# A decoder step's expert stage: dense batches ranked first, one-hot gate groups inside sequences five to eight, last query steps behind the last sequence

## The reference, cut to what matters

```
def block(tb):                                   # 128 tokens
    q = (tb @ wq).reshape(PEER_BLOCK, PEER_HEADS, 2, PEER_QHALF)
    sc = jnp.einsum('thpd,hpnd->thpn', q, keys).astype(jnp.float32)
    s1, i1 = lax.top_k(sc[:, :, 0], PEER_TOPK)
    s2, i2 = lax.top_k(sc[:, :, 1], PEER_TOPK)
    cand = (s1[..., :, None] + s2[..., None, :]).reshape(...)
    cidx = (i1[..., :, None] * PEER_KEYS + i2[..., None, :]).reshape(...)
    top_s, top_p = lax.top_k(cand, PEER_TOPK)
    eidx = jnp.take_along_axis(cidx, top_p, axis=-1)
    g = jax.nn.softmax(top_s, axis=-1)
    act = jax.nn.gelu(jnp.einsum('td,thkd->thk', tb, u_tab[eidx]))
    w = (g * act.astype(jnp.float32)).astype(tb.dtype)
    return jnp.einsum('thk,thkd->td', w, v_tab[eidx])
```

## Time and profile before

| | |
|---|---|
| median of three runs | 3616.84 us (3608.49 to 3617.91) |
| the profiled execution, span | 3614.2 us (its own device time is not given apart from the span) |
| PE busy | 3393.9 us (94%) |
| DVE busy | 2625.2 us (73%) |
| POOL busy | 2070.1 us (57%) |
| ACT busy | 841.3 us (23%) |
| first block of the expert stage | about 672 to 1494 us |
| second block | 1494.67 us to the end |

### The profile page before, as it was taken

One profiled execution on the slowest core, in us unless ns is written; L12 is line 12 of the kernel. 1 busy time (PEld: TensorE's weight loads), 2 busy tenths in 40 slices (PEclk: granted clock), 3 DMA queues, 4 the chain that ended last, 5 costly groups with the idle time before them and its releaser, 6 DMA issues.

```text
span 3614.2 us, 41476 instructions
## 1 busy us (share of the span) xinstructions
PE 3393.9 (94%) x12615; PEld 1771.0 (49%) x12615; DVE 2625.2 (73%) x5427; ACT 841.3 (23%) x1785; POOL 2070.1 (57%) x1636
## 2 busy tenths in 40 slices
PE   8999799899899987999999999999999999999888
PEld 5676564444444444644444444444444444444343
DVE  3344573278777875578887888887888788888884
ACT  2332560244334335311111111111111111111021
POOL 0000100058888888567777777776777677777540
PEclk9999899999999986999999999999999999999999
DMA  4100613478888885999999999999999999999961
GB/s 147 35 23 15 266 75 105 150 196 215 210 217 217 216 208 126 308 366 407 406 406 396 404 404 399 403 393 406 399 400 400 398 389 407 405 404 395 355 215 42
DMA packets 410615, 1023.34 MB, mean 283 GB/s; under 512 B 93965, under 2 KB 130030, under 8 KB 406834
## 3 DMA queue, kind: packets, MB, share of 16 engines
q0 software_dynamic: 221184, 604.27, 46.0%
q1 hardware_dynamic: 175138, 394.69, 31.5%
q10 hardware_dynamic: 14096, 22.02, 1.7%
HBM read 972.05 MB, written 48.77 MB: 282 GB/s over the span
## 4 chain that ended last, share of the span: by engine, by line
DMA 22%; POOL 17%; issue 8%; DVE 7%; PE 4%; ACT 0%; DVEq 0%; SPq 0%; ACTq 0%
DMA u<-in_peer_u,idx_all 21%; POOL v L2134 9%; POOL u L2126 8%; DVE u L2144 2%; DVE facc L2172 2%; PE e_b L2288 1%; PE e_b L2059 1%; DVE wq L2172 1%; PE e_b L2027 1%; DMA w_room<-x_scratch 1%; DVE k_room L2074 1%; PE e_b L2276 0%; DVE ln_st L964 0%; DVE w_room L2358 0%; DVE act L2144 0%
## 5 line engine op out<-in xcount | busy, mean ns | idle before, releaser
L2126 POOL DMA_INDIRECT u<-in_peer_u,idx_all x576 | 727.0, 1262 | 390.8 <-DVE act L2144 260.1
L2059 PE MATMUL e_b<-w_room,e_room 128*128 128x512 f32 x2048 | 910.2, 598 | 24.8 <-DVE k_room L2074 16.3
L2144 DVE CUSTOM_DVE_ANT_0 u<-u,xb 128x1024 f32<-128x1024 f32 x576 | 705.3, 1225 | 299.4 <-DMA u<-in_peer_u,idx_all 291.4
L2027 PE MATMUL e_b<-wq 128*128 128x512 f32 x2048 | 900.4, 592 | 0.0
L2134 POOL DMA_INDIRECT v<-in_peer_v,idx_all x576 | 696.1, 1208 | 216.1 <-issue 174.5
L1756 POOL DMA_INDIRECT gate_scratch<-e_room,slot_of x384 | 611.6, 1593 | 201.8 <-issue 117.5
L2059 PEld LDWEIGHTS e_b<-w_room,e_room 128*128 128x128 f32 x2048 | 391.2, 192 | 524.7 <-issue 491.8
L2027 PEld LDWEIGHTS e_b<-wq 128*128 128x128 f32 x2048 | 379.5, 190 | 429.2 <-issue 429.2
L2172 DVE SCALAR_TENSOR_TENSOR facc<-v,w,facc 128x1024 f32<-128x1024 f32 x317 | 406.6, 1283 | 1.4
L2172 DVE SCALAR_TENSOR_TENSOR wq<-v,w,wq 128x1024 f32<-128x1024 f32 x254 | 325.7, 1282 | 0.5
L2020 ACT ACTIVATE wq<-e_b 128x512 f32<-128x512 f32 x256 | 139.0, 594 | 712.0 <-PE e_b L2013 712.0
(11 more groups left out here) (380 smaller groups left out, 3609.5 us busy)
## 6 DMA issues: line engine op xcount, KB each, us to landing
wq<-in_peer_u SPq DMA_DIRECT2D x128, 512.0 KB, 9.7
w_room<-in_peer_v SPq DMA_DIRECT2D x128, 512.0 KB, 10.3
w_room<-in_cache_k SPq DMA_DIRECT2D x192, 256.0 KB
w_room<-in_cache_v SPq DMA_DIRECT2D x160, 256.0 KB
gate_scratch<-zeros SPq DMA_DIRECT2D x24, 1024.0 KB, 26.6
u<-in_cache_v SPq DMA_DIRECT2D x96, 256.0 KB
wq<-gate_scratch SPq DMA_DIRECT2D x96, 256.0 KB, 16.6
u<-in_cache_k SPq DMA_DIRECT2D x64, 256.0 KB
```

The source lines that it names most:

```text
L2027: last = pe.matmul(AQ[c % 2][:, 0:DT], UT[c % 2][:, k, :], x1Td[:, k, :], start=(k == 0), stop=(k == KC - 1))
L2059: last = pe.matmul(OQ[i % 2][b][:], WT[n % 2][:, c, m * P:m * P + P], Vd[(4 * n + c) % NVD][:, b * 512:b * 512 + 512], start=(c == 0), sto ...
L2126: pool.indirect_dma_start(u[x % NU], None, a["peer_u"], bass.IndirectOffsetOnAxis(ap=idx_all[:, t, h, j:j + 1], axis=0)).then_inc(s_u[x % ...
L2144: dve.tensor_tensor_reduce(u[x % NU], u[x % NU], xb[t % 2][:], 1.0, 0.0, ALU.mult, ALU.add, act16[k % 2][:, j:j + 1]).then_inc(s["ufree"], 1)
```

## The change

The batches are ordered dense first: batches 0 to 7 are the dense group's heads, 8 to 15 the gathering group's, so each batch uses another head's weights and the ring is refilled after every batch. Splitting and quads move from the tail into the sequences with index 4 to 7 (the fifth to the eighth): the split to slot 140, one quad in each of eight slots (20, 22, 23, 25, 26, 28, 29, 31) of each of them, with one PSUM bank and one staging buffer in place of two. In these sequences the q matmuls are thinned to 21, and what is left of them stands in the tail, from `MIXED` to `S_TURN` + 1. The planner gets a room for VectorE of its own in seven slots of the tail. The turned indices take the place of the dense batches' indices in SBUF, no longer of the scores of attention.

```diff
-        jT = S[:, 0:4 * P].rearrange("p (n t) -> p n t", n=4)
-        sqb = S[:, 4 * P:6 * P].rearrange("p (t e) -> p t e", t=2)
+        jT = i_room[0].rearrange("p (n t) -> p n t", n=4)
+        sqb = i_room[1][:, 0:2 * P].rearrange("p (t e) -> p t e", t=2)
...
-        gst = [v_flat[:, n * PK * GB:(n + 1) * PK * GB] for n in (1, 0)]
+        gst = v_flat[:, PK * GB:2 * PK * GB]
...
-        HOT = [B[3], B[7]]
+        HOT = B[3]
...
         def q_pe(pe, e, y):
             m, k = y // KC, y % KC
-            h, group = e // 2, e % 2
+            group = e // PH
             if y == 0:
-                pe.wait_ge(s_wq[h % NR], 16 * (h // NR + 1))
+                pe.wait_ge(s_wq[e % NR], 16 * (e // NR + 1))
...
-            last = pe.matmul(B[m][:], ring[h % NR][:, k, m * P:m * P + P], x1T[group][:, k, :],
+            last = pe.matmul(B[m][:], ring[e % NR][:, k, m * P:m * P + P], x1T[group][:, k, :],
...
-        SPLIT, NQUAD = MIXED, P // 4
-        QUAD_AT, q = {}, 0
-        while q < NQUAD:
-            x = max(QUAD_AT, default=MIXED + 1) + 1
-            n = min(3 if x <= MIXED + 8 else 2, NQUAD - q)
-            QUAD_AT[x] = range(q, q + n)
-            q += n
-        MADE_AT = {x: [q + 2 for q in qs if q + 2 < NQUAD] for x, qs in QUAD_AT.items()}
-        MADE_AT[MIXED + 1] = [0, 1]
+        SPLIT, NQUAD = 4 * SEQ_SLOTS + 12, P // 4
+        QUAD_SLOTS = (20, 22, 23, 25, 26, 28, 29, 31)
+        QUAD_AT, MADE_AT = {}, {SPLIT + 1: [0, 1]}
+        for q in range(NQUAD):
+            x = (SPLIT // SEQ_SLOTS + q // len(QUAD_SLOTS)) * SEQ_SLOTS + QUAD_SLOTS[q % len(QUAD_SLOTS)]
+            QUAD_AT[x] = [q]
+            if q + 2 < NQUAD:
+                MADE_AT[x + 1] = [q + 2]
...
+        Q_LAST = {MIXED: 4, MIXED + 1: 4, O_NORM: 8, O_TURN: 3, O_MIX - 1: 2, O_MIX + 1: 8}
+
+        def q_steps(x):
+
+            c = x % SEQ_SLOTS
+            if x >= MIXED:
+                return Q_LAST.get(x, 0 if x < S_TURN + 1 else 2)
+            if x < 5 or 16 <= c < 20:
+                return 3
+            if x == 6 or c % 8 == 7 or c in (3, 11, 27):
+                return 0
+            if x >= 4 * SEQ_SLOTS:
+                return int(c % 2 == 0 and c < 12 or c in (21, 24, 30))
+            return 1
...
+        DVE_ROOM = {MIXED + 1: 1.5, O_NORM: 0.0, O_TURN: 1.5, O_TURN + 1: 4.0, O_MIX - 1: 4.0, O_MIX: 4.0, O_MIX + 1: 0.0}
...
-                while used + 1.3 * len(MADE_AT.get(slot, ())) >= 2.5 or (slot < MIXED and slot % SEQ_SLOTS in (16, 17)):
+                while (used + 1.3 * len(MADE_AT.get(slot, ())) >= DVE_ROOM.get(slot, 2.5)
+                       or (slot < MIXED and slot % SEQ_SLOTS in (16, 17))):
...
         def scatter_pool(pool, h):
 
-            pool.wait_ge(s["tk"], 2 * h + 1)
+            pool.wait_ge(s["tk"], h + 1)
...
         def split_pe(pe):
-            pe.wait_ge(s["tk"], 2 * (PH - 1) + 1)
-            pe.wait_ge(s["O"], DB)
+            pe.wait_ge(s["tk"], PH)
...
-            wait(pe, s["ge"], q - 1)
-            if q == 1:
-                pe.wait_ge(s["Oe"], DB)
+            wait(pe, s["ge"], q)
...
-                if e % 2 and m:
-                    refill(act, e // 2)
+                if m:
+                    refill(act, e)
```

More of the change, by code:

```diff
@@ L1154, in peer @@
         gd = carve([P, NDT, PH, TOPK])
-        i12d = [carve([P, NDT, PH, TOPK]) for n in range(2)]
+        i_room = [carve([P, NDT * PH * TOPK]) for n in range(2)]
+        i12d = [x.rearrange("p (m h k) -> p m h k", m=NDT, h=PH) for x in i_room]
         i12 = carve([P, 2, UN, TOPK])
@@ L1232, in peer @@
         s_gs = [sem(f"s_gs{n}") for n in range(NSC)]
-        s_gst = [sem(f"s_gst{n}") for n in range(2)]
+        s_gst = sem("s_gst")
         s_xn = [sem(f"s_xn{n}") for n in range(UN)]
@@ L1343, in score_pe @@
                         last = pe.matmul(B[2][:, at:at + PK], qTt[e % 2][:, m, i * P:i * P + P],
-                                         keysT[:, 2 * (e // 2) + m, :], start=True, stop=True)
+                                         keysT[:, 2 * (e % PH) + m, :], start=True, stop=True)
                     else:
@@ L1423, in rank_index_dve @@
                 rule, ids, val = ALU.is_equal, iota[0:R, 0:TOPK], tif[0:R, :, 1, :]
-            dst = i12d[n][:, :, e // 2, :] if e < NBAT and e % 2 == 0 else work(e).i12[0:R, n]
+            dst = i12d[n][:, :, e, :] if e < PH else work(e).i12[0:R, n]
             ch.sync()
@@ L1670, in peer @@
         Q_AT, Q_DONE = {}, {}
+        Q_LAST = {MIXED: 4, MIXED + 1: 4, O_NORM: 8, O_TURN: 3, O_MIX - 1: 2, O_MIX + 1: 8}
[10 more added lines that the diff above has]
+            return 1
         x, step = Q_FIRST, 0
         while step < NBAT * 2 * KC:
-            c = x % SEQ_SLOTS
-            n = 3 if x < 5 or 16 <= c < 20 else 0 if c % 8 == 7 or c in (3, 11, 27) or x == 6 else 1
-            for _ in range(min(n, NBAT * 2 * KC - step)):
+            for _ in range(min(q_steps(x), NBAT * 2 * KC - step)):
                 e, y = step // (2 * KC), step % (2 * KC)
@@ L1806, in quad_pe @@
                 pe.wait_ge(s["jT"], 2)
-            wait(pe, s["ge"], q - 1)
-            if q == 1:
-                pe.wait_ge(s["Oe"], DB)
+            wait(pe, s["ge"], q)
             for t in range(4):
-                last = pe.matmul(HOT[q % 2][:].rearrange("p (e t) -> p t e", t=4)[:, t, :], oh[q % NOH][0][:, t, :],
+                last = pe.matmul(HOT[:].rearrange("p (e t) -> p t e", t=4)[:, t, :], oh[q % NOH][0][:, t, :],
                                  oh[q % NOH][1][:, t, :], start=True, stop=True)
@@ L1817, in quad_act @@
             if n == 0:
-                act.wait_ge(s["qe"], 2 * NBAT)
-                wait(act, s_gst[b % 2], 16 * (b // 2))
+                wait(act, s_gst, 16 * b)
             act.wait_ge(s["gq"], q + 1)
-            dst = gst[b % 2].rearrange("p (e t) -> p e t", t=GB)[:, :, 4 * n:4 * n + 4]
-            act.activation(dst, HOT[q % 2][:].rearrange("p (e t) -> p e t", t=4), ACT.Copy).then_inc(s["ge"], 1)
+            dst = gst.rearrange("p (e t) -> p e t", t=GB)[:, :, 4 * n:4 * n + 4]
+            act.activation(dst, HOT[:].rearrange("p (e t) -> p e t", t=4), ACT.Copy).then_inc(s["ge"], 1)
             if n == GB // 4 - 1:
                 act.wait_ge(s["ge"], q + 1)
-                act.dma_start(rows(hot_d, b * PK, PK), gst[b % 2]).then_inc(s_gst[b % 2], 16)
+                act.dma_start(rows(hot_d, b * PK, PK), gst).then_inc(s_gst, 16)
         def fold_pe(pe):
@@ L1937, in first_act @@
                 act.wait_ge(s["qs"], x - S_Q + 1)
-                refill(act, PH + x - S_Q)
+                refill(act, NBAT + x - S_Q)
             if x in (S_Q + UN, S_Q + 2 * UN):
@@ L1950, in first_act @@
             if x == SPLIT + 1:
-                for q in MADE_AT[x]:
+                for q in (0, 1):
                     quad_hot_act(act, q)
@@ L1995, in load_g @@
             if n == 0:
-                for b in range(2):
-                    sp.wait_ge(s_gst[b], 16 * P // GB // 2)
+                sp.wait_ge(s_gst, 16 * P // GB)
             src = hot_d.rearrange("(b p) (c t) -> p b c t", p=PK, t=GB)[:, :, 4 * n:4 * n + 4, :]
```

7 lines of the change are left out of this document (3 added, 4 removed).

## The result

The changed kernel is slower. Four runs of it gave 3633.29 to 3649.27 us, median 3644.72; four of the kernel before a median of 3617.38. The ratio is 1.0067, with a 95% interval of 1.0050 to 1.0085: 27 us at the medians. The forecast was 3616 with a range to 3630, and "slower by over 0.3%" had a chance of 0.10.

The account below looks back on a forecast made before the run. GpSimd's unbroken chain of 384 scatters was taken to set the second block's start; everything else was hidden before its end, and the start came 0.5 us sooner: 3616.84 - 0.5 gives 3616.3, said as 3616, range 3604 to 3630.

Parts of the forecast that it names:

- I take nothing: Attention sequences: eight more 1 MB weight loads are hidden and cost 0 us; DMA share rises from 0.88 to about 0.92.
- The upper bound of 16 us: Added weight loads: at most 4 us in each of four sequences, if the pages waited for all of it.
- A sequence as now, 81 us; bounds 75 and 85: Sequences with index 4 to 7: quads in and q matmuls out leave each at 81 us, between 75 and 85.
- The last sequence, 81 us at full clock: Last attention sequence: quads and q matmuls bring full clock, so it takes 81 us and ends about 1358 us, not 1371.9.
- T: Time at which attention's last values come: forecast about 1358 us, bounds 1350 and 1380, against 1371.9 before.
- The tail: After attention's last values: VectorE ends 107 to 121 us after T, at 1465 to 1479 us, before the scatters end.
- the 55 us of ranking: End of the tail: VectorE ranks from batch 14's fourth top to batch 15's end, 25.2 + 30.1 us.
- Rival B: Tail: VectorE's ranking of batches 14 and 15 becomes the end if T is over 1372 to 1386; up to 3640 us; chance 0.09.
- The scatters as a floor: End of first block: GpSimd's 384 scatters run without a break to 1486.7 us, so the second block begins at 1494.2 us.

Follow-up runs that it names:

- e1: The kernel before with only the dense-first batch order and a ring load after every batch; quads and q matmuls as before: 3641.3 us, ratio 1.0068.
- e5: e1 without the ring loads after even batches, so one load a sequence as in the kernel before: 3619.2 us, ratio 1.0005.
- e7: The kernel before in its own order, with each head's weights loaded twice, once for each of its two batches: 3634.0 us, ratio 1.0048.
- e3: The changed kernel with all ring loads kept, those after batches 0 to 12 held back to slot 20 or 21 of a sequence: 3627.0 us, ratio 1.0029.
- e6: e1 with all its ring loads kept, those of batches 0 to 12 held back to early in the values half: 3623.6 us, ratio 1.0022.
- e8: The kernel before with 336 of 384 scatters, each head's last two choices left out: 3615.2 us, ratio 0.9996.
- e9: The kernel before with SyncE's last nine issues moved to the head of the second block's SyncE stream: 3613.3 us, ratio 0.9989.
- e4: The changed kernel with the split and the 32 quads back in the tail: 3724.6 us, ratio 1.0294.

## Why the prediction was wrong, by its own steps

**"I take nothing" for the eight loads: the step that failed.** They cost 22 us (e1 - e5) or 16 us (e7 against its own before), and moving them took 18 us off the changed kernel (e3). The working had three parts. That a load lands long before it is needed was right, and beside the point: who waits is not the user of the weights but TensorE, for pages that the load displaces. That the DMA share goes from 0.88 to 0.92 was right to the digit (e6), and it was an average: the share was 0.94 where the load was put and 0.20 after the softmax. The upper bound of 16 us took all eight loads to lie in the first four sequences, as the first eight batches do. But every batch refills the ring, the gathering ones too, so only four of them lie there. The loads in sequences 4 to 6 of the kernel before, of e1 and of the changed kernel:

```profile
wq<-in_peer_wq ACTq DMA_DIRECT2D x3, 1024.0 KB, 9.6
```
```profile
wq<-in_peer_wq ACTq DMA_DIRECT2D x7, 1024.0 KB, 7.9
```
```profile
wq<-in_peer_wq ACTq DMA_DIRECT2D x4, 1024.0 KB, 5.4
```

The rate behind the bound, 4 us a load, would have covered e1: eight loads, 22 us. It was counted for four of them, and then set to nothing.

**"A sequence as now, 81 us; bounds 75 and 85": failed, 89.4.** Of the 25.0 us that sequences 4 to 6 grew, 5.4 go when the loads are moved (e3, 262.7); the changed kernel has only one load more there. The quads and the thinned q table are most of the rest: e3 against e6, which differ in these and the tail's plan, gives 262.7 - 243.9 = 18.8 us in sequences 4 to 6 and 7.0 in sequence 7. TensorE's work is indeed no more (e3 226.7 us busy, e6 226.1). But the prediction looked for the wait in the wrong place: no quad waits for VectorE. TensorE's waits in the changed kernel's sequences 4 to 6:

```profile
PE e_b L1535 <- ACT w_room L1545: 16.3, 21, 3.5
PE e_b L1626 <- ACT w_room L1613: 7.7, 15, 1.5
```

and in the same sequences of the kernel before:

```profile
PE e_b L1535 <- ACT w_room L1545: 5.5, 10, 1.9
...
PE e_b L1626 <- ACT w_room L1613: 3.7, 6, 1.5
```

Attention is a give and take between TensorE and ScalarE: each turned page is copied out before TensorE can go on. The q matmuls were what TensorE did meanwhile. Thinned in the keys half, they leave TensorE waiting for the copies (16.3 for 5.5 us). In the values half there was no room for a quad. Windows of a values half and a keys half before:

```profile
1165.90:1196.30 30.40, 29.48 (x169) 14.48 (x171) 22.21 (x113) 8.44 (x17) 25.52 (x17) 1.00 0.85 207
1196.30:1246.80 50.50, 44.87 (x266) 23.87 (x259) 41.24 (x137) 26.09 (x55) 42.27 (x28) 1.00 0.93 233
```

and after:

```profile
1190.20:1233.00 42.80, 37.80 (x235) 22.95 (x233) 28.12 (x132) 23.84 (x55) 35.78 (x24) 0.92 0.79 194
1233.00:1279.40 46.40, 38.86 (x220) 19.95 (x221) 15.88 (x22) 24.71 (x52) 39.08 (x25) 0.93 0.96 265
```

TensorE was busy for 29.48 of 30.40 us in the values half, so what is added there lengthens it. It grew by 12.4 us: TensorE is busy 8.3 us longer, with eight quads of 1.13 us in, fewer q matmuls and a granted clock of 0.92, and idle 4.1 us longer beside a ScalarE that works three times as much (23.84 for 8.44 us). The keys half, 6 us of TensorE lighter (38.86 for 44.87), gives back 4. The prediction had netted the two halves against each other as if work could flow between them.

**The last sequence, 81 us at full clock: failed.** It took 103 us (1318.26 to 1421.60), with a granted clock of 0.77 in its second half. More work at a better clock took longer than less work at the low one. T came 64 us later than forecast, 1421.6 for 1358, and over 40 past the upper bound.

**The tail: the total right, its parts not.** From T, VectorE was to end after 107 to 121 us; it ended after 111.3 (1532.87). LayerNorm was over at T + 39.8 (forecast 49), the samples' queries were done at T + 89.5. But the 55 us of ranking behind it did not run through. Timeline of ScalarE and VectorE:

```profile
1492.12 0.60 ACT L1357 ACTIVATE e_room<-e_b 128x512 f32<-128x512 f32 x1 [24.26 <-PE e_b L1326]
...
1502.18 0.26 ACT L1437 ACTIVATE e_room<-e_room 128x64 f32<-128x64 f32 x1
...
1502.47 0.22 DVE L1456 TENSOR_REDUCE zx<-e_room 128x4 f32<-128x64 f32 x1 [15.36 <-ACT e_room L1437]
```

VectorE stood 15.4 us for ScalarE's exponentials of batch 14's gates (L1437). ScalarE goes through its slots in order, and ahead of that instruction it had waited 24.3 us for TensorE's sample queries. A LayerNorm that was over 9 us sooner and a wait of 15 us that the forecast did not have offset each other for the most part: that the total came out is in part luck. The tail shrank by 11 us in the changed kernel, and by 20 in e3 against e6, and that is paid for before it starts.

**Rival B named the new end, not what moved T.** It had VectorE's ranking as the last link, from T over 1372 to 1386, at one us for each us, and T went 35 to 50 us past that point. What it gave as the reason, quads that wait for VectorE, did not happen; and e1 loses 24 us with SyncE as its last link. Its largest case was T = 1399. By its own terms that is 1521.5 us and a time of 3644, not the 3640 that it says.

**The scatters as a floor: the last link before, by 1 us.** SyncE issues 13 transfers there, not 12. The last instruction of each engine in the first block is a drain; here are GpSimd's and SyncE's in the kernel before (duration in ns, start in us):

```profile
L2367 POOLq DRAIN  x1: 30178/30178/30178, 1464.2 to 1464.2; - x1
...
L2367 SPq DRAIN  x1: 124/124/124, 1493.3 to 1493.3; - x1
```

GpSimd's ends at 1494.4, 7.7 us behind its last scatter, SyncE's at 1493.4. So the prediction read this execution rightly: two chains within 2 us, the scatters' being the later. But a floor that lies 1 us above another chain gives only that 1 us when it is taken away (e8: 1.2 us of the tail), and it ends nothing once T moves. In the changed kernel GpSimd's drain ended at 1500.5, 33 us ahead of the block. SyncE's chain, the issues behind the queries, moves with T, and it was the last in e1, e5, e6, e7 and e8.

**The sum, from the medians.** Loads 22 (18 by place, 4 by number), order 1 or nothing, quads and thinned table with their shorter tail 3.4 (after - e1) and again 3.4 (e3 - e6). These are differences along one chain of kernels, so they add up to the 27 us by construction. Only the 22 and the 18 are clear of the noise: the intervals of after and e1, of e3 and e6, and of e5 and e6 overlap. In the profiled executions the quads and the table cost 25.8 us in four sequences and return 19.8 in the tail.

**What stays open.** How much of the loads' cost is the displaced pages and how much the clock was not separated by a run; the 5.7 us idle and 3.0 us busy of e1 are one execution. The first four sequences don't show the loads: with those of the kernel before they took 360 us (before) to 367 and 369 us (e5, e8, e9), with doubled ones 366 (e7) and 372 (e1), and with the changed kernel's own 376 (after) and 366 (e4). So differences there were not used, and the wait in sequence 1 is an example and no price. Of e1's 20.7 us over e5 at the second block, 8.7 lie in sequences 4 to 6 and 4.5 in the tail. The scatters' 10 us of added gaps, among them one of 8.3 us with no releaser shown, were not looked into. Nor was a q table tried that keeps its matmuls in the keys half, so quads and thinning have no price each.

## What to carry to other kernels

A transfer "hidden" by its deadline can still cost: look up the DMA share of the very windows in which it will run, not of the stage, and put it into the lull. Likewise work moved into a stage must find idle time of its engine in its own half of the stage; a saving in the other half doesn't pay for it when another engine's copies set the pace there. And to find the last link before a barrier, include the issuing queue's own instructions and each engine's drain; test it by taking the suspected chain away, and look how far behind it the next one stands.

## What was not expected of the hardware

A 1 MB load beside a page stream at a DMA share of 0.94 raised the rate to 357 GB/s for 6 us (231 in the kernel before), and TensorE stood 2.58 us for a page behind it; with the loads moved to where the stream pauses, all eight added ones cost 4 us of the whole time or nothing that shows. And thirteen issues on SyncE's queue took 9.1 us in the kernel before and 9.4 to 10.6 us in e1, e5, e6, e7 and e8, where they set the start of a block on every engine.
